# Five edits to a two-layer transformer step: load order, held-back loads, early sums, convolution banks, w_ada pairs

## The reference

```
for each layer:
    sh1, sc1, g1, sh2, sc2, g2 = silu(cond) @ w_ada + b_ada       # modulation, 6 x 1024 columns
    h    = rms_norm(x) * (1 + sc1) + sh1
    proj = h @ w_in                                               # split among three groups of heads
    mix  = concat(latent attention, 8 heads; convolution module; neighbourhood attention, 4 heads)
    x    = x + g1 * (mix @ w_out)
    h    = rms_norm(x) * (1 + sc2) + sh2
    x    = x + g2 * moe(h)                                        # 16 experts, 2 of them for each token
convolution module: GLU, depthwise convolution of width 31 in time, LayerNorm, silu
expert: (silu(h @ w_gate) * (h @ w_up) * gate) @ w_down           # 1024 -> 512 -> 1024
```

## Time and profile before

| | |
|---|---|
| median of 3 runs | 1071.9 us (1068.68 to 1073.7) |
| the profiled execution | 1071.57 us, its span 1069.8 us |
| TensorE busy | 1006.7 us (94% of the span) |
| VectorE, ScalarE, GpSimd busy | 418.2, 290.9, 143.7 us |
| moved by the DMA engines | 320.52 MB, 300 GB/s over the span |
| turns of layer 0, first row maximum | from 143.04 us |
| out projection of layer 0 | from 238.45 us |
| experts, layer 0 | last down products at 547.64 us |
| out projection of layer 1 | from 731.46 us |
| experts, layer 1 | last down products at 1042.38 us |

### The profile page before, as it was taken

One profiled execution on the slowest core, in us unless ns is written; L12 is line 12 of the kernel. 1 busy time (PEld: TensorE's weight loads), 2 busy tenths in 40 slices (PEclk: granted clock), 3 DMA queues, 4 the chain that ended last, 5 costly groups with the idle time before them and its releaser, 6 DMA issues.

```text
span 1069.8 us, 12824 instructions
## 1 busy us (share of the span) xinstructions
PE 1006.7 (94%) x4770; PEld 593.0 (55%) x4770; DVE 418.2 (39%) x861; ACT 290.9 (27%) x629; POOL 143.7 (13%) x192
## 2 busy tenths in 40 slices
PE   5899898999999999999979999889999999999975
PEld 1686556678854434444338976668874444343422
DVE  1348824586451010000136679767462100101014
ACT  2333265572111011010035337754210111101110
POOL 2200411201110000100101015201020110001000
PEclk9899989999899999999999999978999999999998
DMA  9778396864899999999981225104499999999971
GB/s 376 292 277 342 137 360 274 337 254 195 312 368 362 421 392 422 421 420 422 420 349 57 106 79 163 43 9 197 161 383 391 377 399 423 421 420 422 421 300 59
DMA packets 51376, 320.52 MB, mean 300 GB/s; under 512 B 8718, under 2 KB 8830, under 8 KB 16368
## 3 DMA queue, kind: packets, MB, share of 16 engines
q1 hardware_dynamic: 38448, 276.59, 63.9%
q0 software_dynamic: 12864, 43.08, 10.6%
HBM read 307.08 MB, written 21.25 MB: 307 GB/s over the span
## 4 chain that ended last, share of the span: by engine, by line
PE 76%; DVE 9%; DMA 8%; ACT 3%; issue 2%; POOL 1%; SPq 0%; DVEq 0%; POOLq 0%; ACTq 0%
PE bank L1372 26%; PE bank L1399 12%; PE bank L978 6%; PE bank L1249 5%; PE bank L996 4%; PE bank L961 3%; PE bank L1108 3%; DMA extra_ring<-wring_dram 3%; DMA y<-y_rows 2%; PE bank L1073 2%; PE bank L1039 2%; DMA ring<-wring_dram 2%; PE bank L968 2%; PE bank L1356 2%; PE bank L1285 1%
## 5 line engine op out<-in xcount | busy, mean ns | idle before, releaser
L1372 PE MATMUL bank<-ring,hgT 128*64 128x512 f32 (+1 forms) x512 | 156.4, 594 | 2.1 <-DMA ring<-wring_dram 1.6
L1372 PE MATMUL bank<-extra_ring,hgT 128*64 128x512 f32 (+1 forms) x512 | 155.9, 594 | 0.0
L1399 PE MATMUL bank<-extra_ring,hidT 128*64 128x512 f32 (+1 forms) x352 | 111.8, 624 | 9.7 <-DMA extra_ring<-wring_dram 9.7
L2533 DVE TENSOR_TENSOR sg<-bank,sg 128x512 f32<-128x512 f32 x22 | 15.2, 691 | 252.2 <-PE bank L1372 252.2
L1372 PEld LDWEIGHTS bank<-ring,hgT 128*64 128x64 f32 (+1 forms) x512 | 58.5, 157 | 87.5 <-issue 87.5
L1372 PEld LDWEIGHTS bank<-extra_ring,hgT 128*64 128x64 f32 (+1 forms) x512 | 58.3, 157 | 86.6 <-issue 86.5
L1399 PEld LDWEIGHTS bank<-extra_ring,hidT 128*64 128x64 f32 (+1 forms) x352 | 40.9, 163 | 71.4 <-issue 71.4
L2278 DVE SCALAR_TENSOR_TENSOR conv_acc<-conv_in,vecs,conv_acc 128x399 f32<-128x399 f32 x120 | 70.9, 632 | 2.1
L1108 PE MATMUL bank<-ring,cond_p 128*32 128x512 f32 x384 | 53.3, 675 | 17.0 <-DMA ring<-wring_dram 16.2
L978 PE MATMUL bank<-ring,hT 128*128 128x256 f32 x288 | 66.5, 392 | 2.6 <-DVE hT L1924 2.6
L889 POOL DMA_INDIRECT y_rows<-y,y_at x18 | 18.2, 1011 | 368.2 <-DVE y L2542 348.0
(11 more groups left out here) (315 smaller groups left out, 1532.7 us busy)
## 6 DMA issues: line engine op xcount, KB each, us to landing
ring<-wring_dram SPq DMA_DIRECT2D x150, 1024.0 KB, 12.8
extra_ring<-wring_dram SPq DMA_DIRECT2D x108, 1024.0 KB, 17.8
y_rows<-hg POOLq DMA_DIRECT2D x6, 1024.0 KB, 6.2
kT<-mod_dram POOLq DMA_DIRECT2D x4, 1024.0 KB, 9.8
late<-y_rows POOLq DMA_DIRECT2D x4, 1024.0 KB, 15.5
ring<-wring_dram SPq DMA_DIRECT2D x4, 832.0 KB, 19.5
h_rows<-h_tok POOLq DMA_DIRECT2D x6, 512.0 KB, 6.2
ring<-wring_dram SPq DMA_DIRECT2D x4, 640.0 KB, 11.1
```

Of the source, the lines that this page charges most:

```text
L1372: mm = pe.matmul(b[lo:hi, :], hgT[:, 4 * i + c, lo:hi], in_ring(l, expert_slot(place, s + i))[:, c * 512:(c + 1) * 512], start=((i, c) == ...
L1399: mm = pe.matmul(b[m][lo:hi, :], hidT[:, u % 2, 2 * i + c, lo:hi], in_ring(l, expert_slot(place, 4 + i))[:, at:at + 512], start=((i, c) == ...
```

## The change

Five edits. First, `LOADS` orders the expert loads: all twelve of the two fixed experts first, then the others as in `STREAM`; a slot is given to the next load by the earliest use of what it holds (`USED_AT`). Second, at the start of layer 1 SP waits until the three parts of layer 0 have been read back before it issues any load of layer 1. Third, the six `add_most` stand ahead of the last half of the down products, `down(NU - 1, 1)`, and the closing `add_rows` behind it. Fourth, the last projection stage has one w_ada pair behind it where it had two, and none stands ahead of the heads; turn i has the pair of place 7 + i where it had that of 9 + i, through turn 12. Fifth, the turned convolution takes two banks, one for tiles 0 and 1 and one for tile 2.

```diff
-ADA_BEHIND = (2, 1, 2, 1, 2)
+ADA_BEHIND = (2, 1, 2, 1, 1)
-AMONG_PROJ, BEFORE_HEADS = sum(ADA_BEHIND), 1
+AMONG_PROJ, BEFORE_HEADS = sum(ADA_BEHIND), 0
...
+LOADS = [(k, i) for k in range(FIXED) for i in range(PER_EXPERT)] + [(k, i) for k, i in STREAM if k >= FIXED]
+USED_AT = {ki: a for a, ki in enumerate(STREAM)}
...
-        order += [(n, S_EXP + e * PER_EXPERT + i) for e, i in STREAM]
+        order += [(n, S_EXP + e * PER_EXPERT + i) for e, i in LOADS]
...
-            order += [("cb", t) for t in range(3)]
+            order += [("cb", 0), ("cb", 1)]
...
         else:
-            if j == 0:
+            if left_at is None:
                 cycle = [(base + i) % RING for i in range(RING)] + [RING + i for i in range(EXTRA)]
-            r, j = cycle[j % len(cycle)], j + 1
+                left_at = {r: i - len(cycle) for i, r in enumerate(cycle)}
+            r = min(left_at, key=left_at.get)
+            left_at[r] = USED_AT[divmod(s - S_EXP, PER_EXPERT)]
...
                 l = Layer(n)
+                if n:
+
+                    for t in range(TILES):
+                        sp.wait_ge(parts_loaded[t], 16 * n)
...
-                        for t in range(TILES):
-                            at = 0 if t == 0 else C_LAT - PAD + (t - 1) * P
-                            turn_around(l, ("cb", t), [conv_acc[:, c, at:at + P] for c in range(2)])
+                        for k, ts in enumerate(((0, 1), (2,))):
+                            turn_around(l, ("cb", k), [conv_acc[:, c, CONV_ROWS[t]:CONV_ROWS[t] + P] for t in ts for c in range(2)])
                     if i == 11:
-                        pe.wait_ge(*once_read(l, ("cb", 2)))
+                        pe.wait_ge(*once_read(l, ("cb", 1)))
...
+                    if u == NU - 1:
+                        for t, q in halves:
+                            add_most(t, q)
                     down(u, 1)
...
-                for t, q in halves[:3]:
-                    add_most(t, q)
-                for t, q in halves[:3]:
-                    add_rows(t, q, LAST - 1)
-                for t, q in halves[3:]:
-                    add_most(t, q)
+                for t, q in halves:
                     add_rows(t, q, LAST - 1)
...
+                def turned_conv(t):
+                    dve.wait_ge(*once_full(l, ("cb", t // 2)))
+                    return bank[bank_no(l, ("cb", t // 2))][:, t % 2 * CONV_CH:(t % 2 + 1) * CONV_CH]
...
-                        dve.tensor_scalar(ln_tm[:, t, :], b[:, 0:CONV_CH], meanvar[:, t, 0:1], rstd[:, t:t + 1],
-                                                ALU.subtract, ALU.mult) \
-                                                    .then_inc(bank_read[bank_no(l, ("cb", t))], 1)
+                        ins = dve.tensor_scalar(ln_tm[:, t, :], turned_conv(t), meanvar[:, t, 0:1], rstd[:, t:t + 1],
+                                                ALU.subtract, ALU.mult)
+                        if t:
+                            ins.then_inc(bank_read[bank_no(l, ("cb", t - 1))], 1)
```

More of the change, by code:

```diff
@@ L152 @@
 C_OUT = C_LEN - 2 * PAD
+CONV_ROWS = (0, C_LAT - PAD, C_LAT - PAD + P)
 TAPS_BEFORE_LATENTS, TAPS_BEFORE_UP, TAPS_BEFORE_HEADS = 7, (18, 8), (21, 14)
@@ L337, in slots_by_turn @@
     last = [None] * (RING + EXTRA)
-    j = 0
+    left_at = None
     for q, (n, s) in enumerate(RING_ORDER):
         if s < S_EXP:
-            r, base, j = base % RING, base + 1, 0
+            r, base, left_at = base % RING, base + 1, None
         else:
-            if j == 0:
+            if left_at is None:
                 cycle = [(base + i) % RING for i in range(RING)] + [RING + i for i in range(EXTRA)]
-            r, j = cycle[j % len(cycle)], j + 1
+                left_at = {r: i - len(cycle) for i, r in enumerate(cycle)}
+            r = min(left_at, key=left_at.get)
+            left_at[r] = USED_AT[divmod(s - S_EXP, PER_EXPERT)]
         at.append((r, taken[r]))
@@ L349, in slots_by_turn @@
         taken[r] += 1
-        if s >= S_EXP and j == NE * PER_EXPERT:
-            base = cycle[0]
+        if s >= S_EXP and (q + 1 == len(RING_ORDER) or RING_ORDER[q + 1][0] != n):
+            base = min(range(RING), key=left_at.get)
     return at, before
@@ L1436, in _ @@
                 list_rows(0)
+                halves = [(t, q) for t in range(TILES) for q in range(2)]
                 gate_or_up(0, "G", 0, sems["gate_half"])
@@ L1467, in _ @@
                         pe.wait_ge(*once_read(l, (f"turned{i}",)))
+                    for t, q in halves:
+                        pe.matmul(bank[bank_no(l, (f"A{t}{q}",))][:, :], iden[:], parts[t][:, 0, 512 * q:512 * (q + 1)], start=False, stop=True)
                     with pe.Fori(0, extra) as w:
@@ L1495, in _ @@
                             pe.wait_ge(more_y_made[n], w * NE + (e + 1))
-                halves = [(t, q) for t in range(TILES) for q in range(2)]
-                for t, q in halves[:3]:
-                    add_most(t, q)
-                for t, q in halves[:3]:
-                    add_rows(t, q, LAST - 1)
-                for t, q in halves[3:]:
-                    add_most(t, q)
+                    for t, q in halves:
+                        add_most(t, q)
+                for t, q in halves:
                     add_rows(t, q, LAST - 1)
@@ L2354, in normalise_conv @@
                     for t in range(TILES):
-                        dve.wait_ge(*once_full(l, ("cb", t)))
-                        b = bank[bank_no(l, ("cb", t))]
-                        dve.tensor_scalar(ln_tm[:, t, :], b[:, 0:CONV_CH], meanvar[:, t, 0:1], rstd[:, t:t + 1],
-                                                ALU.subtract, ALU.mult) \
-                                                    .then_inc(bank_read[bank_no(l, ("cb", t))], 1)
+                        ins = dve.tensor_scalar(ln_tm[:, t, :], turned_conv(t), meanvar[:, t, 0:1], rstd[:, t:t + 1],
+                                                ALU.subtract, ALU.mult)
+                        if t:
+                            ins.then_inc(bank_read[bank_no(l, ("cb", t - 1))], 1)
                 for i in range(len(GROUPS) + 2):
@@ L2400, in _ @@
                         for t in range(TILES):
-                            dve.wait_ge(*once_full(l, ("cb", t)))
-                            b = bank[bank_no(l, ("cb", t))]
-                            dve.bn_stats(stats[:, t, :], b[:, 0:CONV_CH]).then_inc(sems["dve_step"], 1)
+                            dve.bn_stats(stats[:, t, :], turned_conv(t)).then_inc(sems["dve_step"], 1)
                             dve.wait_ge(sems["dve_step"], step(l))
```

## The result

| | before | after |
|---|---|---|
| median | 1072.8 us, 4 runs | 1089.01 us, 4 runs |
| lowest to highest | 1068.68 to 1075.29 | 1083.09 to 1094.17 |
| ratio, 95% interval | | 1.0146 [1.0102, 1.0189] |
| the profiled execution, its span | 1071.57, 1069.8 us | 1090.79, 1088.7 us |

A forecast was written before the change was run, and what follows sets the result against it. TensorE led the chain (76% of the span), with limits differing by stage. Terms 0 + 2.1 - 4.3 + 0.8 + 1.3 = -0.1 on 1071.57 gave 1071.5, stated as 1072 us; range 1064 to 1081.

The forecast's parts named there:

- The w_ada pairs: Layer 0's turns: early lead lost at out0's late load and cast; out products at 240.5 against 238.45, +2.1 us.
- the hole: Layer 0, before the scores of turn 11: TensorE has nothing to do from about 216 to 222.2 us.
- the distance of the sum: Layer 0: scores of group 10 to first out product, 30.4 us in the prediction's working without the clock (240.5 less 210.1).
- the hole at out0 costs the clock: Layer 0, turns 11 to 13: the idle TensorE drops to the lower clock, +6 us, hence 1078; chance 0.27.
- 240.5: Forecast start in us of layer 0's out products, against 238.45 before.
- The fixed experts' loads: Expert stage: head start of two loads ends against full slots; 0 forecast, between 0 and -5.1 us per layer.
- The hold-back: End of layer 0: with layer 1's loads held, the last part lands near 548.4 instead of 554.12; held loads stay hidden.
- The convolution: Layer 1, turns 10 and 11: scores of turn 11 start 2.7 us early and run at full clock, 1.6 more: -4.3 us.
- The rival in which the whole clock comes back: Layer 1's lower-clock stretch runs at full clock, -7 us, and layer 0 loses nothing: 1066; chance 0.13.
- The sums: Layer ends: last down product waits behind sums needing the last part; +0.8 us in layer 0, +1.3 in layer 1.
- the +6 worked out for layer 0: End of layer 0: cost if holding loads back speeds nothing and the last part stays at 554.12, in place of +0.8.
- the two slow rivals: Clock lost at layer 0's hole (1078, chance 0.27), and last down product waiting for a late part (1077, chance 0.06).

The follow-up runs named there:

- busy_hole2: After, plus idle products in layer 0: 24 ahead of the scores of turn 11, 8 ahead of the last group, on a bank already read; ratio 1.0025.
- hold_only: Before, plus only the holding back of layer 1's loads until layer 0's parts are read back; ratio 0.9988.
- conv_only: Before, plus only the convolution in two banks; ratio 0.9956.
- pairs_only: Before, plus only the move of the w_ada pairs; ratio 1.0083, median 1082.32 us.
- sums_only: Before, plus only the six sums ahead of the last half of the down products; ratio 1.0089.
- loads_only: Before, plus only the new order of expert loads and choice of slots; ratio 1.0001.
- two_old_pairs: After, with only two sums early and the w_ada pairs and out casts of layer 0 in their old places; ratio 0.9870, 1060.49 us.

## Why the prediction was wrong, point by point

**The w_ada pairs: the step that failed.** Priced at +2.1 us, it measured +12.85 to the first gate product in the profiled execution, and 0.83% alone. Its mechanism was right almost to the instruction up to the hole: the cast of out0 at 219.9 (219.45 measured), the scores of turn 11 at 222.2 (221.64), the last group behind ScalarE's copy. The step that failed is that every row behind the hole was taken at full clock, where the granted clock was 0.50 for 13.66 us. With the clock kept up by idle products the out products came 30.5 us behind the scores of group 10, the distance of the sum; with the clock as it fell, 38.6. That the first agrees to 0.1 us is partly luck: in busy_hole2 the casts of out2 and out3 stood behind ScalarE's own work and waited for no load, where the sum had them wait for their loads. The working had the hole of 6 us in its own text, and the row of a wait of 2.93 us followed by 17.07 us at 0.50 beside it. The first rival, "the hole at out0 costs the clock", was the case that came, but at 0.27 it had too little chance, and at +6 too little price. It counted turns 11 to 13 alone. Of the 7.5 us by which the out products missed 240.5, 4.4 are the load of out3, issued at 233.93 where the sum had 229.5, since its slot is freed by a pair that came late and ran at half speed; 2.6 are that load, which took 8.9 us to land where the sum had 6.3, and no run tells why; 0.7 are the transposes of the last group at the lower clock; the casts between took 0.3 less than counted. The last group waited 5.11 us, and a second stretch at 0.50 reached into the out products. A third, from 291.21 to 301.45, stood at 0.50 ahead of the experts, where before 6.83 us did.

**The fixed experts' loads:** nothing, as forecast (1.0001). **The hold-back:** the part landed 0.6 us later than forecast in hold_only, and alone it changed the time by nothing that shows, as expected.

**The convolution:** -4.3 forecast, -0.44% measured alone (4.7 us of 1078, between 1 and 8.4), and 2.8 us by the traces. The rival in which the whole clock comes back did not occur, and the scores did not come at full clock either (2.81 us).

**The sums:** +0.8 and +1.3 forecast; in after 2.5 and 3.1. The terms were right in kind and too small. In layer 0 the second part was late too (1.64 us of wait at 561.86), and the last part landed near 562.7, 1.4 us later than 548.4 with the 12.85 of the stage added; in layer 1 the weighing ended on time and the clock fell behind the wait: the two sums took 4.35 us (1061.54 to 1065.89) where the working had 2.64. The working for layer 1 also left out the 0.3 us ahead of the first closing sum that it counts in layer 0. Without the hold-back the +6 worked out for layer 0 was 6.5 to 8.6.

**The sum and the range:** the parts measured alone, 0.83 - 0.44 + 0.89 + 0.01 - 0.12, add up to 1.17%, and the whole is 1.46% with an interval that holds it. No effect between the edits is shown, though the intervals of five parts leave room for some 0.8%. The upper end of 1081 left out the two slow rivals together; what came was the first at a higher price, and a greater loss by the sums than forecast.

## What to carry to other kernels

When a moved load lets one engine stand before a cast, look at what else is queued behind that cast, and price the hole on TensorE with the clock: here a hole of 6 us was followed by 13.66 us at the lower level, and filling it with idle products won back 1.2%. Ahead of a product whose weights come last, put only work whose own inputs have landed by then: with two sums early and the pairs in their old places the kernel was 1.3% faster than before, with six 0.2% slower, an interval that holds zero. And a wait removed at one end of a chain can come back at the other: eleven us of lead were lost again before the cast of out0. Moving the casts took that loss away, but a gain from the pairs themselves was not shown.

## What the runs showed of the hardware

The clock at 0.50 held through work without a gap: in conv_only TensorE was busy for all of the 10.24 us from 712.68 on, with scores, transposes and value products, at the lower level. With idle products of 128x128 in the hole ahead of the same kind of work, in busy_hole2, it stood at 1.00 for the 18 us that followed, where it was 0.50 for 13.66 us without them.

Single executions of one kernel differ in the clock. The time at the lower level in the turns of layer 1 was 10.24, 17.07, 17.07, 20.48 and 37.55 us in the profiled executions of pairs_only, before, sums_only, loads_only and hold_only, whose program is the same there. The six executions of two_old_pairs had a mean granted clock of 0.973 to 0.977 at 1059 to 1061.5 us and 0.960 and 0.961 at 1067.3 and 1069.7. So a stage that is compared in two single traces can be off by several us by the clock alone; the table of lateness above is such a comparison, and the ratios carry the argument.
